# Three pairs of modulation products move to other PSUM banks beside the index and attention scores

## The reference, cut to what matters

```python
mod = silu(c) @ w_ada + b_ada                     # 6 rows of 1024: shift1, scale1, gate1, shift2, scale2, gate2
h = rms_norm(x) * (1 + scale1) + shift1
q_a, k_a, v_a, q_i, k_i, w_i, q_r, k_r, v_r, g_r = split(h @ w_in)
score = sum_heads(w_i * relu(q_i @ k_i.T))        # index, 8 heads
att = softmax over the 128 keys with the best score   # attention, 8 heads
ret = silu(g_r) * rms_norm(retention(q_r, k_r, v_r))
x = x + gate1 * rms_norm([att, ret] @ w_out, g_post_mix)
h2 = rms_norm(x, g_pre_ffn) * (1 + scale2) + shift2
x = x + gate2 * rms_norm(moe(h2), g_post_ffn)     # top 1 of 4 groups, top 2 of 8 experts
```

## Time and profile before

| what | value |
|---|---|
| median of three runs | 696.54 us |
| the profiled execution's own time | 696.76 us |
| its span, first to last instruction | 694.9 us |
| TensorE busy | 633.0 us, 91% |
| VectorE busy | 375.2 us, 54% |
| ScalarE busy | 207.0 us, 30% |
| GpSimd busy | 100.5 us, 14% |
| bytes moved | 174.70 MB, mean 251 GB/s |

### The profile page before, as it was taken

One profiled execution on the slowest core, in us unless ns is written; L12 is line 12 of the kernel. 1 busy time (PEld: TensorE's weight loads), 2 busy tenths in 40 slices (PEclk: granted clock), 3 DMA queues, 4 the chain that ended last, 5 costly groups with the idle time before them and its releaser, 6 DMA issues.

```text
span 694.9 us, 7089 instructions
## 1 busy us (share of the span) xinstructions
PE 633.0 (91%) x2400; PEld 298.1 (43%) x2400; DVE 375.2 (54%) x721; ACT 207.0 (30%) x411; POOL 100.5 (14%) x96
## 2 busy tenths in 40 slices
PE   0499998999899999999979999989999999988793
PEld 0365443444344444455544457433434453433231
DVE  5936574999977675316983336872332333232046
ACT  3344433334245444441121223111212221221023
POOL 1004332320033222000000000112111111110001
PEclk9999999999999999999999997999999999999997
DMA  9990906070602507071099119799999999999996
GB/s 313 394 373 17 342 11 242 1 242 0 240 4 51 192 16 289 1 247 34 1 370 396 80 60 367 265 371 411 421 419 420 420 419 420 419 416 414 408 408 141
DMA packets 52757, 174.70 MB, mean 251 GB/s; under 512 B 9712, under 2 KB 9712, under 8 KB 41840
## 3 DMA queue, kind: packets, MB, share of 16 engines
q1 hardware_dynamic: 45136, 160.26, 59.6%
q0 software_dynamic: 6160, 12.10, 5.5%
q10 hardware_dynamic: 1424, 1.87, 0.8%
HBM read 168.43 MB, written 15.21 MB: 264 GB/s over the span
## 4 chain that ended last, share of the span: by engine, by line
PE 69%; DVE 15%; DMA 4%; issue 4%; SPq 4%; ACT 2%; DVEq 0%; ACTq 0%; POOLq 0%
PE psum L768 16%; PE psum L1048 13%; PE psum L771 8%; PE psum L916 7%; PE psum L1109 7%; SPq L540 4%; DMA ring<-in_w_up_exp 2%; DVE work L1454 2%; DVE score L1525 2%; DVE sm L1524 2%; DVE score L1755 2%; PE psum L1021 2%; PE psum L831 2%; PE psum L901 2%; DVE rows L1454 2%
## 5 line engine op out<-in xcount | busy, mean ns | idle before, releaser
L768 PE MATMUL psum<-hT,ring 128*128 128x512 f32 (+1 forms) x320 | 135.4, 578 | 0.0
L1048 PE MATMUL psum<-ring,hT 128*64 128x512 f32 (+2 forms) x320 | 93.9, 618 | 4.0 <-DMA ring<-in_w_up_exp 3.7
L768 PEld LDWEIGHTS psum<-hT,ring 128*128 128x128 f32 x320 | 60.2, 192 | 69.9 <-issue 60.6
L771 PE MATMUL psum<-ring,hT 128*128 128x512 f32 x192 | 85.2, 597 | 0.0
L1243 ACT ACTIVATE both_bufs<-psum 32x512 f32<-32x512 f32 (+2 forms) x68 | 38.4, 564 | 77.8 <-PE psum L768 77.2
L1873 DVE TENSOR_SCALAR work<-work 128x256 f32<-128x256 f32 x16 | 4.6, 290 | 100.3 <-PE psum L1058 74.5
L1454 DVE SCALAR_TENSOR_TENSOR rows<-ring,sm,rows 128x512 f32<-128x512 f32 x64 | 55.5, 866 | 1.7
L771 PEld LDWEIGHTS psum<-ring,hT 128*128 128x128 f32 x192 | 35.6, 190 | 44.6 <-issue 44.2
L1048 PEld LDWEIGHTS psum<-ring,hT 128*64 128x64 f32 (+2 forms) x320 | 32.2, 145 | 52.3 <-issue 48.9
L1342 ACT ACTIVATE work<-psum 128x256 f32<-128x256 f32 x17 | 6.5, 384 | 149.2 <-PE psum L1048 149.2
L1109 PE MATMUL psum<-ring,work 128*64 128x512 f32 (+1 forms) x160 | 40.1, 598 | 0.7 <-ACT work L1348 0.7
(11 more groups left out here) (319 smaller groups left out, 914.7 us busy)
## 6 DMA issues: line engine op xcount, KB each, us to landing
ring<-in_w_down_exp SPq DMA_DIRECT2D x20, 1024.0 KB, 18.6
ring<-in_w_in SPq DMA_DIRECT2D x8, 2048.0 KB, 9.1
ring<-in_w_ada SPq DMA_DIRECT2D x8, 2048.0 KB, 13.7
ring<-in_w_gate_exp SPq DMA_DIRECT2D x14, 1024.0 KB, 20.2
ring<-in_w_up_exp SPq DMA_DIRECT2D x14, 1024.0 KB, 22.9
ring<-in_w_ada SPq DMA_DIRECT2D x7, 1024.0 KB, 14.6
ring<-in_w_gate_exp SPq DMA_DIRECT2D x12, 512.0 KB, 15.3
ring<-in_w_up_exp SPq DMA_DIRECT2D x12, 512.0 KB, 15.8
```

Source lines behind the costliest of these rows:

```text
L768: mm = pe.matmul(o[:, at], w[:, k, b * P:(b + 1) * P], hT3[:, k, at], start=(k == 0), stop=(k == KD - 1))
L771: mm = pe.matmul(o[:, :], hT3[:, k, b * P:(b + 1) * P], w[:, k, :], start=(k == 0), stop=(k == KD - 1))
L1048: mm = pe.matmul(o[rows, :], XT[u % 2][:, k, rows], both(GU_SLOT[place])[:, k, :, :], start=(k == 0), stop=(k == KD - 1))
```

## The change

MOD 2 takes banks 2 and 3. MOD 3 and MOD 4 take bank 7 for the first product and the next bank of `score` for the second. No instruction of an engine is added or removed.

```diff
             if s in ("ka", "va", "kr") and b == NB - 1:
                 m = {"ka": 2, "va": 3, "kr": 4}[s]
-                score(("MOD", m, 0), False)
-                score(("MOD", m, 1), False)
+                if m == 2:
+                    use(("MOD", m, 0), 2)
+                    use(("MOD", m, 1), 3)
+                else:
+                    use(("MOD", m, 0), 7)
+                    score(("MOD", m, 1), False)
                 step("MOD", m)
```

## The result

The changed kernel took 686.73 us (median of 4 runs, 685.86 to 688.92) against 696.66 us for the kernel before (4 runs): ratio 0.986, 95% interval 0.981 to 0.990. Two further comparisons gave 0.990 (0.988 to 0.992) and 0.987 (0.983 to 0.991). Over all comparisons the mean of 16 runs of the changed kernel is 687.1 us, and that of 117 runs of the kernel before is 695.7: 8.6 us, with a standard error of 0.5.

What follows compares the result with a forecast made beforehand. TensorE's order was taken to bound the stage of the change. Terms of 4.05, 2.30 and 0.74 made 7.09 us, less 0.85 for the clock's uncertainty 6.2, so 696.76 became 690.5 us; range 687.8 to 694.2.

Steps and rivals of the forecast that it cites:

- MOD 2: In front of its products: the 2.35 us stop and 1.70 us of half clock behind it go, gain 4.05 us.
- MOD 3: Stop cut by 0.86 us to 1.57, 1.69 us of half clock saved, 0.25 us wait deducted: gain 2.30 us.
- MOD 4: The first product, on bank 7, covers the stop of 0.74 us, with no clock lost: gain 0.74 us.
- VectorE follows: Between MOD 2 and MOD 3: VectorE's whole stream moves 4.05 us earlier, at no cost.
- The new wait: Behind MOD 3, index head (3,7) waits for VectorE's copy of the second product, delayed by key selection: 0.25 us lost.
- How sure the clock is: At the long stops: half clock follows in three of four cases, so 0.85 us comes off 7.09, leaving 6.2.
- The sum: Over the stage: 4.05 + 2.30 + 0.74 = 7.09 us off the profiled 696.76, giving 689.67 us.
- falls luckier: Behind the stage, the stop at 361.38 or at 454 us turns out better: a larger gain, chance 0.03.
- Rival A: At the MOD stops: the clock does not hang on them, only 3.95 us of standing goes, 692.8 us; chance 0.14.
- Rival B: Downstream, at the start of the experts' stream: two thirds of the gain are given back, 694.4 us; chance 0.09.
- C: Expert stage: its DMA stream runs slower; above 2.9% the whole gain is lost, at 6% 704.3 us; chance 0.04.
- D: At the products' bank waits: these were not what came last, so the booking changes nothing, 696.8 us; chance 0.03.

Runs made afterwards that it cites:

- the filled stop: Kernel before with two extra unread matmuls in front of the wait at MOD 2 and at MOD 3, all waits kept: 694.65 us, ratio 0.998.
- the control: Kernel before, unchanged, run against itself for another profile: 696.09 us, ratio 1.000.
- the second control: Kernel before, unchanged, run against itself once more for a third profile: 694.46 us, ratio 0.998.

## Why the prediction was right or wrong

- **MOD 2**: right, 4.08 us for 4.05, both halves of it: 2.35 of standing and 1.70 of clock, the latter by the filled stop.
- **VectorE follows**: right. The read that lets MOD 3 go on came 4.13 us earlier (L831 from 180.66 in the control, 176.53 here); the stop left at MOD 3 is the 1.28 us that VectorE's lateness leaves, 0.29 less than the forecast 1.57, because two passes alone take 1.13 us where 0.86 were counted.
- **MOD 3**: right in size, 2.43 us for 2.30. The new wait was there, at the place named, but for another reason than the one given. The prediction had head (3,7) wanted half of 1.13 us behind head (3,6). In the control's trace the two start 0.01 us apart, so the wait is 0.77 us; only 0.12 of it reached the next unit, for the 0.25 assumed.
- **MOD 4**: right, 0.79 for 0.74.
- **How sure the clock is**: this step failed by some 0.6 us. The three in four that it took from four stops were borne out at 10 in 13, but it let the two stops at MOD count as independent and took 0.85 us off. In the two profiles where the first stop left the clock up, the second cost 2.84 and 2.82 instead of 1.7. The mean price over five profiles is 3.16 of 3.39, so 0.2 us were to be taken off.
- **The step that failed most**: "The sum" has no term for the half clock outside the stage. The prediction knew the case (a stop further on that "falls luckier") and gave it a chance of 0.03 and no price. Outside the two stops the half clock fell by some 3.8 us a run, up to 1.9 us of time; by the means 1.5 us of the gain are in no term. Together with 0.2 us that the three terms came out larger and the 0.6 above this is the way from 6.2 to 8.6. Why those 1.5 us came with the change is not shown; set against the second control's profile, the changed kernel's has nothing beyond the terms.
- **The range**: its low end was 8.7 us under the median, and the first comparison gave 10.0. Single executions of the kernel before differ with a standard deviation of 1.8 us, and a median of 3 or 4 of them on either side carries about 1.5 us into the difference (an estimate from that deviation); about 1 us was allowed in all. The first comparison's 10.0 us were in part luck: over all runs it is 8.6.
- **The base**: the profile it rested on had lost 1.9 us ahead of MOD 2, with half clock at 42 us, which the two controls did not have. This did no harm to the terms, which are differences within it.
- Rival A is refuted by the filled stops, and with it the rule of the Trainium skill ("TensorE: Matmul & The Clock Gate", "A second HAM failure mode: psum-queue depth-cycling") is no account of this stage: banks are cycled as before, pauses of 0.6 us remain, and the changed kernel's clock is 1.00 in all five windows from 102 to 260 us. Rival B is refuted: the load moved by 7.2 us against one control and 7.4 against the other, and the last matmul by 8.7 and 7.3. C and D did not occur.

## What to carry to other kernels

Where an in-order engine takes a fresh result bank, ask who read that bank last and how late that reader is; a bank whose reader was done long ago turns a stop into nothing without touching the work. Count the half clock behind a stop of 2 us or more as part of its price (here 1.7 us on 2.35), and check it by filling the stop with matmuls that nobody reads. Do not take the prices of two such stops as independent: here the second cost 2.8 us where the first had cost nothing. And do not expect to add up such gains to the microsecond: two kernels with a shorter stage were no faster.

## What was not expected of the hardware

Two neighbouring index heads, on partitions 0 to 63 and 64 to 127, run side by side: in the control their passes start 0.01 us apart and both heads take 1.13 us together. In the changed kernel the second starts at 185.23, 0.05 us behind the end of VectorE's read at 185.18, and the pair takes 1.90 us. The 0.77 more are that wait.

The granted clock behind the same stop differs between executions and between kernels that are alike up to there. A stop of 1.28 us cost it once and left it up in the changed kernel's three profiles; full stops of 2.34 to 2.41 us left it up three times in thirteen. The stop of 2.31 us near 357 us left it up in the three profiles of the kernel before and cost it in the two with work added behind that stop.
